# Delta-rule units on one Trainium2 core: masked reads, turns and reads as 64 by 64 products

## The chip, the cores and the metric

The kernel runs on one core of one Trainium2 chip. The metric is the device time of one execution in microseconds; the figure given is the median of several runs. A core has TensorE (matrix products, PE in the profile), VectorE (DVE), ScalarE (ACT), GpSimd (POOL) and SyncE (SP), which here only issues transfers. Products go to PSUM, which has 8 banks of 512 float32 columns on 128 partitions; VectorE and ScalarE carry them on to SBUF.

## The reference

Two blocks follow each other on 1024 tokens of width 1024: a first block (state space mixer, stick-breaking attention, feed-forward) and a second one, whose mixer has a gated linear attention with 4 heads and a delta rule with 8 heads of width 64. The change touches the delta rule:

```python
def _rwkv7_scan(r, decay, k, v, kk, a):
    def step(S, inp):
        r_t, w_t, k_t, v_t, kk_t, a_t = inp
        sa = jnp.einsum('bhvk,bhk->bhv', S, -kk_t)
        S = (S * w_t[:, :, None, :]
             + sa[..., None] * (kk_t * a_t)[:, :, None, :]
             + v_t[..., None] * k_t[:, :, None, :])
        y = jnp.einsum('bhvk,bhk->bhv', S, r_t)
        return S, y
```

After it come, per head, mean and variance over the 64 values of y, a normalisation, a bonus and a gate, and then the product of all heads with `w_out_2`, a residual and a last norm.

## The kernel before, in words

The function `rwkv_units_phase` computes the delta rule and what follows. The 1024 tokens are 8 units of 128, and a unit is two sub-blocks of 64 tokens (`SUB`). A head h = a * 4 + q stands on the partitions of half a (`half(h)`), at place q; `sub(k)` are the partitions or columns of sub-block k. A unit's inputs are five kinds of tiles, read from `parked_units` into `held(c)`: the read vectors (RT_KIND), keys (KT_KIND), removal keys in two forms (KAP_KIND, BT_KIND) and values (VV_KIND), each with channels on partitions and tokens in columns. The inverses of the unit's triangular matrices were made earlier and are fetched into `xt` and `x11`.

One loop, with c from -1 to 7, finishes unit c and prepares unit c + 1; below, pass c is one round of it. The order on each engine is the order of the code, and semaphores connect the engines. On TensorE a pass is:

- `read_values(c)` (line 3574): values times masked reads `rk` into the output sum `y_ps`, bank 6
- `removals(c+1)` (3503): 32 products of 64 by 64 into banks 2 and 3
- `reads_of_removed(c+1)` (3496): 8 products of 128 by 128 (contraction 64) of BT with RT into banks 0 and 1. VectorE multiplies all 128 by 128 entries with a mask (`incl2`) that keeps only the two diagonal 64 by 64 blocks and their causal part, and writes `rb`
- `removal_maps(c)` (3581, 3588): the state's removal map, and `rr_ps` in bank 7
- `turn_values(c+1)` (3527), `reads_of_keys(c+1)` (3496): transposes of keys and values into banks 2 and 3; products of KT with RT, masked into `rk`
- `values(c)` (3595, 3598, 3602): the new states' parts, and the reads of removed values into bank 6
- `means(c-1)` (3627), `turn_keys(c+1)` (3527), `key_parts(c+1)` (3546, 3550)
- `recur(c, 0)` (3614, 3619), `corner(c+1)` (3557), `variances(c-1)` (3631), `recur(c, 1)`, `removed(c+1)` (3566)

Float32 products of four array quarters are possible because a 64 by 64 product takes one half of the rows (partitions of the operands) and one half of the columns (partitions of the result). In the trace a float32 product is two matmul records, a transpose one.

VectorE in a pass: `front` (3699 mask of removals `ak`, 3704 mask `rb`), `maps` (3712, 3717), `front_keys` (3708), `deviation` (3733), `keys` (3722, 3724), `key_values` (3728), the two state updates (3757) with `corner` (3764) between, `result(c-1)` (3741, 3745, 3747), and in passes 1 to 4 `gated(c-1)` (3751, 3753), two operations of 1024 columns for the linear attention's heads. ScalarE: high halves of finished outputs (3831, 3852), copies out of PSUM (3855, 3859, 3868, 3875, 3878), squares (3835) and the root of the variance as logarithm and exponential (3840, 3842). GpSimd makes low halves of outputs (3486, 3478) and cuts the output weights in two (3465 to 3469).

Behind the loop come the output products (3674 to 3676), in three spans of tokens.

Of the kernel before, what the change touches and what calls it, by code (L numbers as in the profile page):

```python
# [14 lines left out]
P = 128  # L15
# [3332 lines left out]
def rwkv_units_phase(nc, S, D, W, plast, L, spare, ssq, merged, parked_h, back, out, s_result, first_unit, s_first):  # L3348
# [6 lines left out]
    with Phase(nc) as ctx:  # L3355
# [11 lines left out]
        rb = part(flat, 4 * SEQ, 2 * SEQ).rearrange("p (s h n) -> p s h n", s=2, h=H)  # L3367
        rk = part(flat, 6 * SEQ, SEQ).rearrange("p (h n) -> p h n", h=H)
# [27 lines left out]
        (s_zero, s_clear, s_rb, s_ak, s_rk, s_zt, s_bt, s_kvt, s_q, s_akv, s_dx, s_w, s_g, s_rr, s_gs, s_yd,  # L3396
         s_rbm, s_akm, s_rkm, s_aam, s_z0, s_tokb, s_tokv, s_qm, s_z1, s_x, s_nw, s_gc, s_rrc, s_state, s_y, s_h, s_hy) = (sem(n) for n in (
            "zero", "clear", "rb", "ak", "rk", "zt", "bt", "kvt", "q", "akv", "dx", "w", "g", "rr", "gs", "yd",
# [17 lines left out]
        y_cols = lambda h: slice((h % RWKV_P) * P, (h % RWKV_P + 1) * P)  # L3416
# [3 lines left out]
        with nc.Block() as block:  # L3420
# [71 lines left out]
            def _(pe):  # L3492
                def wide_products(c, key, kind, out):

                    for h in ORDER:
                        last = nc.tensor.matmul(out[:, h * P:(h + 1) * P], held(c)[half(h), key, h % RWKV_P, :], held(c)[half(h), kind, h % RWKV_P, :],  # L3496
                                                start=True, stop=True)
                    return last
# [18 lines left out]
                def reads_of_removed(c):  # L3517
                    pe.wait_ge(s_nw, c)
                    wide_products(c, BT_KIND, RT_KIND, low_ps).then_inc(s_rb, 1)

                def reads_of_keys(c):
                    pe.wait_ge(s_rbm, c + 1)
                    wide_products(c, KT_KIND, RT_KIND, low_ps).then_inc(s_rk, 1)

                def turned(c, b, kind):
                    for p in range(RWKV_P):
                        last = nc.tensor.transpose(bank(b)[:, p * P:(p + 1) * P], held(c)[:, kind, p, :], S.ident[:, :])  # L3527
                    return last

                def turn_values(c):  # L3530
                    pe.wait_ge(s_akm, c + 1)
                    pe.wait_ge(s_aam, c + 1)
                    turned(c, 2, KT_KIND)
                    turned(c, 3, VV_KIND).then_inc(s_kvt, 1)
# [26 lines left out]
                def removed(c):  # L3561
                    pe.wait_ge(s_x, c + 1)
                    pe.wait_ge(s_z1, c + 1)
                    pe.wait_ge(s_tokb, c + 1)
                    for h in ORDER:
# [4 lines left out]
                def read_values(c):  # L3570
                    pe.wait_ge(s_rkm, c + 1)
                    pe.wait_ge(s_y, c)
                    for h in ORDER:
                        nc.tensor.matmul(y_ps[half(h), y_cols(h)], tkv[:, c % 2, 1, h % RWKV_P, h // RWKV_P, :], rk[:, h, :], start=first(h), stop=False)

                def removal_maps(c):
# [8 lines left out]
                    if c >= 2:  # L3585
                        pe.wait_ge(s_ln, c - 1)
                    for h in ORDER:
                        last = nc.tensor.matmul(rr_ps[half(h), y_cols(h)], nw[:, h, 0, :], rb[:, s, h, :], start=True, stop=True)
                    last.then_inc(s_rr, 1)

                def values(c):
# [9 lines left out]
                    for h in ORDER:  # L3601
                        last = nc.tensor.matmul(y_ps[half(h), y_cols(h)], nw[:, h, 1, :], rb[:, s, h, :], start=False, stop=False)  # L3602
                    last.then_inc(s_hy, 1)

                def recur(c, k):
# [11 lines left out]
                    for h in ORDER:  # L3617
                        at = (h % RWKV_P) * P + k * SUB
                        last = nc.tensor.matmul(y_ps[half(h), at:at + SUB], st[half(h), k, h % RWKV_P, :], rr[half(h), h % RWKV_P, sub(k)],
                                                start=False, stop=(k == 1 and last_(h)))  # L3620
# [3 lines left out]
                def means(c):  # L3624
                    pe.wait_ge(s_y, c + 1)
                    pe.wait_ge(s_rrc, min(c + 2, NUNIT))
                    nc.tensor.matmul(rr_ps, S.same[:, :], y[:, c % 2, :, :].rearrange("p q n -> p (q n)"), start=True, stop=True).then_inc(s_mean, 1)  # L3627

                def variances(c):
                    pe.wait_ge(s_sq, c + 1)  # L3630
                    nc.tensor.matmul(rr_ps, S.same[:, :], sq[:, :, :].rearrange("p q n -> p (q n)"), start=True, stop=True).then_inc(s_var, 1)  # L3631

                for c in range(-1, NUNIT):
# [49 lines left out]
                means(NUNIT - 1)  # L3683
                pe.wait_ge(s_glo, GLA_HEADS)
# [10 lines left out]
            def _(dve):  # L3695
                def front(c):
# [7 lines left out]
                    nc.vector.tensor_tensor(rb[:, s, :, :], by_head(low_ps), S.incl2[:, :].unsqueeze(1).to_broadcast([P, H, P]), ALU.mult).then_inc(s_rbm, 1)  # L3704

                def front_keys(c):
                    dve.wait_ge(s_rk, c + 1)
                    nc.vector.tensor_tensor(rk, by_head(low_ps), S.incl2[:, :].unsqueeze(1).to_broadcast([P, H, P]), ALU.mult).then_inc(s_rkm, 1)

                def maps(c):  # L3710
# [6 lines left out]
                    nc.vector.tensor_tensor(rr[:, :, :], rr_ps.rearrange("p (q n) -> p q n", q=RWKV_P), held(c)[:, RT_KIND, :, :], ALU.add).then_inc(s_rrc, 1)  # L3717
# [369 lines left out]
```

## Time and profile before

| | |
|---|---|
| median of 3 runs | 2276.01 us (2269.75 to 2276.87) |
| the profiled execution | 2273.69 us |
| its span | 2271.9 us, 43790 instructions |
| TensorE busy | 2167.5 us (95%) |
| VectorE busy | 1574.2 us (69%) |
| ScalarE busy | 993.5 us (44%) |
| mean granted clock of TensorE | 0.987 of 2.4 GHz |
| the unit loop | about 2006 to 2173 us of the span |

Busy time is the sum of what an engine executed; matmuls are pipelined, so a busy TensorE can still be one that works below its peak. What bounds a stretch is read from the chain of waits: from the last instruction back, at each step, to whatever released it. "issue" there is time in which the engine waited for nothing that the profile shows.

### The profile page before, as it was taken

Reading aid. Unit: us, or ns where it says so; the run is one execution under the profiler, and the core shown is the slowest. Engines: PE = TensorE matmul, PEld = TensorE weight load, DVE = VectorE, ACT = ScalarE, POOL = GpSimd, SP = SyncE. Lnnn points to the kernel's source line nnn. Section 1 sums busy time; section 2 is a strip of 40 time slices with the busy share of each in tenths; the row PEclk is TensorE's granted clock in tenths of the full one; section 3 lists DMA queues with packets and bytes.
Section 4 is the critical chain, followed back from the end, with each engine's and each line's share of the span. In section 5 each row is a group of like instructions: output and inputs, shape, how many; then the busy total and the mean of one; then the engine's idle time right before and its main releaser. Section 6 shows DMA issues by size and latency. Waiting matters only on the chain. (4 is left out here: it accounts for less than half of the span.)

```text
span 2271.9 us, 43790 instructions
## 1 busy us (share of the span) xinstructions
PE 2167.5 (95%) x18260; PEld 1377.7 (61%) x18260; DVE 1574.2 (69%) x2017; ACT 993.5 (44%) x1739; POOL 605.8 (27%) x379
## 2 busy tenths in 40 slices
PE   7999989999999899899999999999999999989998
PEld 4666665556666566566666665448644445568746
DVE  6876887988888755787777774247787576246654
ACT  3226765666666543524444443235553332224321
POOL 3555673100000220073333331000155532101160
PEclk9999999999999999999999999999999999999999
DMA  3113214667777632111111113326424522033412
GB/s 133 47 56 96 83 66 75 132 131 141 147 136 147 135 105 77 44 56 42 56 57 57 57 53 120 102 68 208 139 90 125 167 93 89 14 98 99 167 61 75
DMA packets 287947, 218.32 MB, mean 96 GB/s; under 512 B 203328, under 2 KB 253696, under 8 KB 286352
## 3 DMA queue, kind: packets, MB, share of 16 engines
q1 hardware_dynamic: 287760, 215.64, 34.9%
q8 instruction: 139, 2.28, 0.4%
q14 instruction: 48, 0.39, 0.1%
HBM read 145.77 MB, written 25.76 MB: 75 GB/s over the span
## 5 line engine op out<-in xcount | busy, mean ns | idle before, releaser
L1499 DVE TENSOR_TENSOR_SCAN att_left<-att_left,att_unseen_prefix 16x16 f32<-16x16 f32 (+5 forms) x144 | 175.5, 1258 | 16.6 <-ACT att_left L1327 16.4
L2886 PE MATMUL ps<-second_x_hi,whi_z 128*128 128x512 f16 (+1 forms) x480 | 179.2, 373 | 2.6 <-DVE second_x_lo L1714 1.4
L1221 PE MATMUL ps<-x_hi,whi_z 128*128 128x348 f16 x560 | 175.8, 314 | 4.4 <-DVE att_q L1431 4.4
L2888 PE MATMUL ps<-second_x_hi,wlo_z 128*128 128x512 f16 (+1 forms) x480 | 178.9, 373 | 0.0
L2887 PE MATMUL ps<-second_x_lo,whi_z 128*128 128x512 f16 (+1 forms) x480 | 178.8, 373 | 0.0
L1223 PE MATMUL ps<-x_hi,wlo_z 128*128 128x348 f16 x560 | 174.7, 312 | 0.0
L1222 PE MATMUL ps<-x_lo,whi_z 128*128 128x348 f16 x560 | 174.5, 312 | 0.0
L1341 ACT ACTIVATE att_left_split<-att_left 128x256 f16<-128x256 f32 (+7 forms) x128 | 87.3, 682 | 142.1 <-DVE att_left L1499 128.1
L2189 PE MATMUL ps<-x_lo,whi_z 128*128 128x342 f16 x432 | 133.2, 308 | 0.0
L2188 PE MATMUL ps<-x_hi,whi_z 128*128 128x342 f16 x432 | 132.9, 308 | 0.0
L2190 PE MATMUL ps<-x_hi,wlo_z 128*128 128x342 f16 x432 | 132.7, 307 | 0.0
L2855 POOL TENSOR_TENSOR wlo_z<-wraw_z,whi_z 128x1024 f16<-128x1024 f32 x28 | 65.9, 2354 | 180.0 <-ACT whi_z L3071 180.0
L1456 DVE SCALAR_TENSOR_TENSOR att_left_split<-att_left,att_left_split 128x256 f16<-128x256 f32 (+7 forms) x128 | 96.9, 757 | 0.2
L3071 ACT ACTIVATE whi_z<-wraw_z 128x1024 f16<-128x1024 f32 x28 | 29.6, 1056 | 133.5 <-PE ps L2888 117.1
L219 PE MATMUL ps<-x_hi,whi_xbc 128*128 128x348 f16 x264 | 82.6, 313 | 4.6 <-DVE x_lo L487 4.6
L2886 PEld LDWEIGHTS ps<-second_x_hi,whi_z 128*128 128x128 f16 x480 | 46.9, 98 | 62.3 <-issue 6.5
L1268 PE MATMUL ps<-att_left_turned,att_v_tokens 128*64 128x128 f16 x1728 | 64.4, 229 | 19.7 <-DMA att_left_turned<-att_left_split 10.2
L221 PE MATMUL ps<-x_hi,wlo_xbc 128*128 128x348 f16 x264 | 82.5, 312 | 0.0
L220 PE MATMUL ps<-x_lo,whi_xbc 128*128 128x348 f16 x264 | 82.4, 312 | 0.0
L1327 ACT ACTIVATE att_left<-ps 16x16 f32<-16x16 f32 (+5 forms) x144 | 79.1, 595 | 4.4 <-PE ps L1237 4.4
L1221 PEld LDWEIGHTS ps<-x_hi,whi_z 128*128 128x128 f16 x560 | 54.5, 97 | 43.2 <-issue 15.6
L2887 PEld LDWEIGHTS ps<-second_x_lo,whi_z 128*128 128x128 f16 x480 | 47.0, 98 | 53.7 <-issue 3.9
(655 smaller groups left out, 6226.5 us busy)
## 6 DMA issues: line engine op xcount, KB each, us to landing
wraw_z<-in_w_second SPq DMA_DIRECT2D x30, 512.0 KB, 4.1
wraw_z<-in_w_up SPq DMA_DIRECT2D x26, 512.0 KB, 3.6
wraw_z<-in_w_qkv SPq DMA_DIRECT2D x24, 512.0 KB, 4.5
wraw_z<-in_w_down SPq DMA_DIRECT2D x20, 512.0 KB, 3.5
raw_down<-in_w_down SPq DMA_DIRECT2D x20, 512.0 KB, 4.1
seg<-dt_a_sums SPq DMA_DIRECT2D x18, 512.0 KB, 5.3
wraw_z<-in_w_up SPq DMA_DIRECT2D x36, 256.0 KB, 3.3
second_work<-parked_units SPq DMA_DIRECT2D x7, 1280.0 KB, 7.3
```

What stands on the lines that cost most here:

```text
L1221: nc.tensor.matmul(lin_ps(g), hi, xhi, start=(kb == 0), stop=False)
L1222: nc.tensor.matmul(lin_ps(g), hi, xlo, start=False, stop=False)
L1223: last = nc.tensor.matmul(lin_ps(g), lo, xhi, start=False, stop=(kb == DB - 1))
L1341: last = nc.scalar.activation(left_part(e, 0, P * t.j), of_head(t, a, 0, P * t.j), ACT.Copy, scale=PSCALE)
L1456: last = nc.vector.scalar_tensor_tensor(low_, of_head(t, a, 0, P * t.j), PSCALE, high, ALU.mult, ALU.subtract)
L1499: nc.vector.tensor_tensor_scan(x, x, unseen, 1.0, ALU.mult, ALU.max).then_inc(s_scan, 1)
L2188: nc.tensor.matmul(out, hi, xhi, start=begin, stop=False, skip_group_check=True)
L2189: nc.tensor.matmul(out, hi, xlo, start=False, stop=False, skip_group_check=True)
L2190: of_block = nc.tensor.matmul(out, lo, xhi, start=False, stop=stop, skip_group_check=True)
L2886: nc.tensor.matmul(out, hi, xhi, start=(j == 0), stop=False)
L2887: nc.tensor.matmul(out, hi, xlo, start=False, stop=False)
L2888: return nc.tensor.matmul(out, lo, xhi, start=False, stop=(j == DB - 1))
```

## The change

All large products of the unit loop that had a dimension of 128 become 64 by 64 products, and results move to other banks.

- The masked reads (`own_products` in place of `wide_products`) compute only the two diagonal 64 by 64 blocks of each head: 16 calls in place of 8, into the low half of banks 0 and 1, and the masks on VectorE work on 512 columns in place of 1024.
- The turns are products with an identity of 64 by 64, 16 calls in place of 4 transposes, both kinds side by side in the same two banks.
- `read_values`, the `rr` part of `removal_maps` and the reads of removed values (now `read_removed`) contract over one sub-block, 16 calls in place of 8. `y_ps` and `rr_ps` share banks 6 and 7, one bank for each sub-block.
- Means and variances go to banks 0 and 1 (bank 7 for the last unit). So the turns of the keys wait for the deviation, the variances for the copy of the turned keys, and `removed` for the logarithm.
- In a pass `reads_of_keys` stands ahead of `turn_values`, and the means ahead of `read_removed`.

```diff
-        low_ps, high_ps = (S.ps[:, b:b + 2, :].rearrange("p a n -> p (a n)") for b in (0, 2))
+        low_ps = S.ps[:, 0:2, :].rearrange("p a n -> p (a n)")
+        own_ps = S.ps[:, 0:2, 0:RWKV_P * SUB].rearrange("p a (q n) -> p a q n", n=SUB)
+        turned_ps = lambda b, j: S.ps[:, b:b + 2, j * RWKV_P * SUB:(j + 1) * RWKV_P * SUB].rearrange("p a (q n) -> p a q n", n=SUB)
...
-        y_ps, rr_ps = bank(6), bank(7)
+        y_ps, rr_ps = (S.ps[:, 6:8, o * RWKV_P * SUB:(o + 1) * RWKV_P * SUB].rearrange("p k (q n) -> p k q n", n=SUB) for o in range(2))
+        mean_ps, var_ps = (lambda c, b=b: bank(7 if c == NUNIT - 1 else b) for b in range(2))
...
-                def wide_products(c, key, kind, out):
-
-                    for h in ORDER:
-                        last = nc.tensor.matmul(out[:, h * P:(h + 1) * P], held(c)[half(h), key, h % RWKV_P, :], held(c)[half(h), kind, h % RWKV_P, :],
-                                                start=True, stop=True)
+                def own_products(c, key, kind):
+
+                    for k, h in kh:
+                        last = nc.tensor.matmul(own_ps[sub(k), h // RWKV_P, h % RWKV_P, :], held(c)[half(h), key, h % RWKV_P, sub(k)],
+                                                held(c)[half(h), kind, h % RWKV_P, sub(k)], start=True, stop=True)
                     return last
...
-                def turned(c, b, kind):
-                    for p in range(RWKV_P):
-                        last = nc.tensor.transpose(bank(b)[:, p * P:(p + 1) * P], held(c)[:, kind, p, :], S.ident[:, :])
+                def turned(c, b, j, kind):
+                    for k, h in kh:
+                        last = nc.tensor.matmul(turned_ps(b, j)[sub(k), h // RWKV_P, h % RWKV_P, :], held(c)[half(h), kind, h % RWKV_P, sub(k)],
+                                                S.ident[half(h), half(h)], start=True, stop=True)
                     return last
...
                 def turn_keys(c):
                     pe.wait_ge(s_rkm, c + 1)
-                    turned(c, 0, KAP_KIND).then_inc(s_zt, 1)
-                    turned(c, 1, BT_KIND).then_inc(s_bt, 1)
+                    if c >= 2:
+                        pe.wait_ge(s_dev, c - 1)
+                    turned(c, 0, 0, KAP_KIND)
+                    turned(c, 0, 1, BT_KIND).then_inc(s_bt, 1)
...
-                    for h in ORDER:
-                        nc.tensor.matmul(y_ps[half(h), y_cols(h)], tkv[:, c % 2, 1, h % RWKV_P, h // RWKV_P, :], rk[:, h, :], start=first(h), stop=False)
+                    for k, h in kh:
+                        nc.tensor.matmul(y_ps[half(h), k, h % RWKV_P, :], tkv[sub(k), c % 2, 1, h % RWKV_P, h // RWKV_P, :], rk[sub(k), h, :],
+                                         start=first(h), stop=False, skip_group_check=True)
...
+                def read_removed(c):
+                    pe.wait_ge(s_rrc, c + 1)
+                    for k, h in kh:
+                        last = nc.tensor.matmul(y_ps[half(h), k, h % RWKV_P, :], nw[sub(k), h, 1, :], rb[sub(k), c % 2, h, :], start=False, stop=False,
+                                                skip_group_check=True)
                     last.then_inc(s_hy, 1)
...
                 def means(c):
                     pe.wait_ge(s_y, c + 1)
-                    pe.wait_ge(s_rrc, min(c + 2, NUNIT))
-                    nc.tensor.matmul(rr_ps, S.same[:, :], y[:, c % 2, :, :].rearrange("p q n -> p (q n)"), start=True, stop=True).then_inc(s_mean, 1)
+                    if c + 2 < NUNIT:
+                        pe.wait_ge(s_rkm, c + 3)
+                    nc.tensor.matmul(mean_ps(c), S.same[:, :], y[:, c % 2, :, :].rearrange("p q n -> p (q n)"), start=True, stop=True).then_inc(s_mean, 1)
...
                     if ahead:
+                        reads_of_keys(c + 1)
                         turn_values(c + 1)
-                        reads_of_keys(c + 1)
                     if now:
-                        values(c)
+                        new_states(c)
                     if c >= 1:
                         means(c - 1)
+                    if now:
+                        read_removed(c)
```

The places of instructions on TensorE, first before. This is the middle of a pass with c of 2 or more, from `read_values` to `key_parts`; `second_work` holds the unit's inputs, `z` stands for `rb`, `rk`, `nw` or the removal tile, `ffn_out` for `tkv` and `xt`.

```order
L3574 MATMUL ps<-z,ffn_out 64x128 x8
L3503 MATMUL ps<-second_work 64x64 x32
L3496 MATMUL ps<-second_work 128x128 x8
L3581 MATMUL ps<-ru_tok_removal,z 64x64 x16
L3588 MATMUL ps<-z 64x128 x8
L3527 MATMUL ps<-ident,second_work 128x128 x8
L3496 MATMUL ps<-second_work 128x128 x8
L3595 MATMUL ps<-ffn_out 64x64 x16
L3598 MATMUL ps<-z,ru_tok_removal 64x64 x16
L3602 MATMUL ps<-z 64x128 x8
L3627 MATMUL ps<-wraw_z,same_chunk 128x512
L3527 MATMUL ps<-ident,second_work 128x128 x8
```

Every second group stands at another tile shape than the one ahead of it, and the read of the keys stands behind the turn of the values. The same place on TensorE in the changed kernel:

```order
L3582 MATMUL ps<-z,ffn_out 64x64 x16
L3506 MATMUL ps<-second_work 64x64 x32
L3499 MATMUL ps<-second_work 64x64 x16
L3590 MATMUL ps<-ru_tok_removal,z 64x64 x16
L3595 MATMUL ps<-z 64x64 x16
L3499 MATMUL ps<-second_work 64x64 x16
L3530 MATMUL ps<-ident,second_work 64x64 x32
L3603 MATMUL ps<-ffn_out 64x64 x16
L3606 MATMUL ps<-z,ru_tok_removal 64x64 x16
L3639 MATMUL ps<-wraw_z,same_chunk 128x512
L3613 MATMUL ps<-z 64x64 x16
L3530 MATMUL ps<-ident,second_work 64x64 x32
```

All but the means have one tile shape; the read of the keys (the second 3499) moved ahead of the turn of the values, and the means (3639) ahead of the reads of the removed values (3613). VectorE's order is the same, with two operations half as wide.

## Rows read from the trace of the kernel before

**Rows 1.** The page: busy time, share and instructions of the engines.
```profile
PE 2167.5 (95%) x18260; PEld 1377.7 (61%) x18260; DVE 1574.2 (69%) x2017; ACT 993.5 (44%) x1739; POOL 605.8 (27%) x379
```

**Rows 2.** Stretches: length, busy and instructions per engine, clock, DMA share, GB/s.
```profile
2084.30:2104.20 19.90, 19.03 (x436) 16.18 (x436) 13.86 (x25) 9.12 (x13) 3.46 (x3) 1.00 0.35 99
...
2124.80:2149.80 25.00, 22.72 (x458) 19.38 (x460) 12.95 (x25) 7.11 (x10) 2.82 (x2) 0.93 0.78 288
```

**Rows 3.** The chain that ended last, one unit: start, us, engine, what.
```profile
2095.70 0.70 ACT ru_y_rs L3840
...
2101.35 1.24 DVE second_work L3753
...
2104.29 0.74 PE ps L3527 x5
```

**Rows 4.** Timeline of TensorE in one unit: start, us, engine, line, operation, tiles.
```profile
2105.29 1.16 PE L3496 MATMUL ps<-second_work 64*128 64x128 f32 x16
...
2106.38 0.69 PE L3595 MATMUL ps<-ffn_out 64*64 64x64 f32 x32
...
2107.47 1.09 PE L3602 MATMUL ps<-z 128*64 128x128 f32 x16
...
2108.49 1.13 PE L3627 MATMUL ps<-wraw_z,same_chunk 128*128 128x512 f32 x2
...
2109.46 1.04 PE L3527 MATMUL ps<-ident,second_work 128*128 128x128 f32 x8
...
2110.42 1.12 PE L3546 MATMUL ps<-ffn_out,ru_removal 64*64 64x32 f32 x32
...
2118.39 1.09 PE L3574 MATMUL ps<-z,ffn_out 128*64 128x128 f32 x16
...
2119.41 1.16 PE L3503 MATMUL ps<-second_work 64*64 64x64 f32 x64
...
2120.51 1.16 PE L3496 MATMUL ps<-second_work 64*128 64x128 f32 x16
...
2121.60 0.69 PE L3581 MATMUL ps<-ru_tok_removal,z 64*64 64x64 f32 x32
...
2122.22 1.09 PE L3588 MATMUL ps<-z 128*64 128x128 f32 x16
...
2124.88 1.07 PE L3527 MATMUL ps<-ident,second_work 128*128 128x128 f32 x8 [1.56 <-ACT ru_removal L3855]
```

**Rows 5.** The same timeline, two of VectorE and one of ScalarE.
```profile
2109.66 0.69 DVE L3733 SCALAR_TENSOR_TENSOR wraw_z<-ps,wraw_z 128x512 f32<-128x512 f32 x1 [1.94 <-PE ps L3627]
...
2115.44 0.69 ACT L3840 ACTIVATE ru_y_rs<-ps,gn_eps 128x512 f32<-128x512 f32 x1 [3.46 <-PE ps L3631]
...
2123.08 0.68 DVE L3699 TENSOR_TENSOR ru_ak<-ps,excl 128x512 f32<-128x512 f32 x1
```

**Rows 6.** Waits of TensorE from 2020 to 2172 us: total, times, longest.
```profile
PE ps L3614 <- issue: 1.8, 2, 1.4
```

**Rows 7.** Timeline of TensorE at the longest stall.
```profile
2145.01 0.46 PE L3581 MATMUL ps<-ru_tok_removal,z 64*64 64x64 f32 x16 [2.03 <-issue]
```

**Rows 8.** Half-microsecond stretches: length, TensorE busy, clock, DMA share, GB/s.
```profile
2146.50:2147.00 0.50, 0.50 (x4) 0.50 0.29 107
...
2149.00:2149.50 0.50, 0.50 (x8) 0.50 0.00 0
```

**Rows 9.** Timeline: first unit, and the ScalarE step behind two later variances.
```profile
2015.02 1.12 PE L3546 MATMUL ps<-ffn_out,ru_removal 64*64 64x32 f32 x32
...
2136.03 0.69 ACT L3840 ACTIVATE ru_y_rs<-ps,gn_eps 128x512 f32<-128x512 f32 x1 [3.46 <-PE ps L3631]
...
2159.16 0.69 ACT L3840 ACTIVATE ru_y_rs<-ps,gn_eps 128x512 f32<-128x512 f32 x1 [3.46 <-PE ps L3631]
```

**Rows 10.** Timeline behind the last unit: VectorE held up, GpSimd later.
```profile
2181.27 2.93 DVE L3741 SCALAR_TENSOR_TENSOR wraw_z<-wraw_z,params,ru_y_rs 128x128 f32<-128x128 f32 x4 [3.65 <-ACT ru_y_rs L3842]
...
2186.84 1.16 POOL L3486 TENSOR_TENSOR second_x_lo<-wraw_z,second_x_hi 128x512 f16<-128x512 f32 x1 [3.58 <-ACT second_x_hi L3831]
```

More of the change, by code:

```diff
@@ L3366, in rwkv_units_phase @@
         tkv = mid_w.rearrange("p (s j q a n) -> p s j q a n", s=2, j=2, q=RWKV_P, a=2)
-        rb = part(flat, 4 * SEQ, 2 * SEQ).rearrange("p (s h n) -> p s h n", s=2, h=H)
-        rk = part(flat, 6 * SEQ, SEQ).rearrange("p (h n) -> p h n", h=H)
+        rb = part(flat, 4 * SEQ, SEQ).rearrange("p (s h n) -> p s h n", s=2, h=H)
+        rk = part(flat, 5 * SEQ, SEQ // 2).rearrange("p (h n) -> p h n", h=H)
         nw = part(flat, 7 * SEQ, SEQ).rearrange("p (h a n) -> p h a n", h=H, a=2)
@@ L3584, in removal_maps, with new_states @@
                     pe.wait_ge(s_rrc, c)
[L3585 to L3588, printed above, removed]
+                    for k, h in kh:
+                        last = nc.tensor.matmul(rr_ps[half(h), k, h % RWKV_P, :], nw[sub(k), h, 0, :], rb[sub(k), s, h, :], start=False, stop=True,
+                                                skip_group_check=True)
                     last.then_inc(s_rr, 1)
-                def values(c):
+                def new_states(c):
                     s = c % 2
@@ L3600, in values @@
                     last.then_inc(s_h, 1)
-                    for h in ORDER:
-                        last = nc.tensor.matmul(y_ps[half(h), y_cols(h)], nw[:, h, 1, :], rb[:, s, h, :], start=False, stop=False)
+                def read_removed(c):
+                    pe.wait_ge(s_rrc, c + 1)
+                    for k, h in kh:
+                        last = nc.tensor.matmul(y_ps[half(h), k, h % RWKV_P, :], nw[sub(k), h, 1, :], rb[sub(k), c % 2, h, :], start=False, stop=False,
+                                                skip_group_check=True)
                     last.then_inc(s_hy, 1)
@@ L3617, in recur @@
                     for h in ORDER:
-                        at = (h % RWKV_P) * P + k * SUB
-                        last = nc.tensor.matmul(y_ps[half(h), at:at + SUB], st[half(h), k, h % RWKV_P, :], rr[half(h), h % RWKV_P, sub(k)],
-                                                start=False, stop=(k == 1 and last_(h)))
+                        last = nc.tensor.matmul(y_ps[half(h), k, h % RWKV_P, :], st[half(h), k, h % RWKV_P, :], rr[half(h), h % RWKV_P, sub(k)],
+                                                start=False, stop=last_(h), skip_group_check=True)
                     if k:
@@ L3625, in means @@
                     pe.wait_ge(s_y, c + 1)
-                    pe.wait_ge(s_rrc, min(c + 2, NUNIT))
-                    nc.tensor.matmul(rr_ps, S.same[:, :], y[:, c % 2, :, :].rearrange("p q n -> p (q n)"), start=True, stop=True).then_inc(s_mean, 1)
+                    if c + 2 < NUNIT:
+                        pe.wait_ge(s_rkm, c + 3)
+                    nc.tensor.matmul(mean_ps(c), S.same[:, :], y[:, c % 2, :, :].rearrange("p q n -> p (q n)"), start=True, stop=True).then_inc(s_mean, 1)
                 def variances(c):
                     pe.wait_ge(s_sq, c + 1)
-                    nc.tensor.matmul(rr_ps, S.same[:, :], sq[:, :, :].rearrange("p q n -> p (q n)"), start=True, stop=True).then_inc(s_var, 1)
+                    if c + 2 < NUNIT:
+                        pe.wait_ge(s_tokb, c + 3)
+                    nc.tensor.matmul(var_ps(c), S.same[:, :], sq[:, :, :].rearrange("p q n -> p (q n)"), start=True, stop=True).then_inc(s_var, 1)
                 for c in range(-1, NUNIT):
```

41 lines of the change are left out of this document (23 added, 18 removed).

## The prediction, as it was put on record

> **What bounds the kernel now.** I read the page first, then the table of stretches, then the chain of waits, then the timeline of one unit on each engine. The page says that TensorE is busy 95% of the span [rows 1], but the change touches only the last loop over eight units, some 165 us of 2271.9. In a stretch of one unit TensorE is busy 19.03 of 19.90 us and VectorE 13.86 [rows 2], so one would call it bound by TensorE. The chain says otherwise for some units. Unit by unit there are two cases.
>
> In loop passes 2 to 5 (pass c works on unit c and prepares unit c+1) the chain leaves TensorE. It goes from ScalarE's logarithm of the variance (line 3840) at 2095.70 through VectorE's normalising and its two wide operations for the other head family (3751, 3753), which end at 2102.59, through the mask of the next unit and a ScalarE copy, back to TensorE at 2104.29 [rows 3]. The next logarithm starts at 2115.44 [rows 5], so the loop is 19.74 us: 8.59 away from TensorE, 11.15 on it. TensorE idles before line 3527 in these passes, 1.56 us in one [rows 4]. In passes 0, 1 and 6 the wide operations don't stand there, and TensorE sets the pace. So a saving on TensorE counts in full in three passes, and in four only where it lies between line 3527 and the variances.
>
> **The price of a product.** In rows 4 the start of one group to the start of the next is what a group costs. 32 calls on 64 by 64 quarters (3503) go from 2119.41 to 2120.51, 1.10 us; 16 such calls (3581) from 2121.60 to 2122.22, 0.62 us. The difference is 0.48 us for 16 calls, and 0.14 us is left for the change of tile shape ahead of each. Eight wide calls cost about twice that: 3496 takes 1.09, 3602 takes 1.02, 3574 takes 1.02 [rows 4].
>
> **TensorE, part by part, per unit.** Reads of values and removals after them: 2118.39 to 2120.51, 2.12, become 0.14 + 0.48 + 0.96 = 1.58, saves 0.54. Masked read of removals (3496): 1.09 to 0.48, saves 0.61. The maps (3581) lose their shape change, 0.14. Line 3588, 1.02 back to back as 3602 is, to 0.48, saves 0.54. Masked read of keys: 1.09 to 0.48, saves 0.61. Turns: eight transposes at 128 by 128 took 1.00 (2104.29 to 2105.29) and 0.96 (2109.46 to 2110.42); 32 calls of a quarter cost 0.96, saves 0.04 and nothing. States (3595 and 3598): 1.09 to 0.96, saves 0.13. Line 3602: 1.02 to 0.14 + 0.48, saves 0.40. The sum is 3.0 us of 19 per unit [rows 3, 4].
>
> The Trainium skill's page TensorEngine Tiling (Array Packing), section Instruction Overhead, says that each matmul carries about 60 cycles, so that a dimension of 64 gains nothing by being cut. As an estimate by that page, 32 records of 25 ns would make a group 0.80 us instead of 0.48, and nearly all of the 3.0 us would be gone over nine such groups. The trace disagrees: 0.48 us for a group of 32 records.
>
> **The wait that is added.** Means now write bank 0, which the turns of the keys write next, so those turns wait for VectorE's deviation. From the start of the means to the start of the deviation is 1.17 us (2108.49 to 2109.66) and it lasts 0.69 [rows 4, 5], with a hop of 0.06 in all 1.92. TensorE has 0.97 of means and 0.62 of reads in that time, 1.59, and then waits 0.33. Queued behind are the turns and all that follows in the pass. The other new waits are covered: the means' wait for the masked keys (VectorE is two operations of 0.68 ahead by then, against 1.9 us of turns and states), the variances' for a copy that ends over 2 us earlier, the removal product's for the logarithm (0.69, under the recurrence's 0.93 beside it); if that last cover went, it would cost 0.3 us a pass, and I count that in the low end.
>
> **VectorE and ScalarE.** The two masks fall from 1024 to 512 columns; a mask of 512 takes 0.68 [rows 5]. In the passes that TensorE bounds they are hidden either way. In the others the first is on the path now, since the read of the keys is put ahead of the turn and waits for it. The evictions that only change their stride keep their element count; I take them at no change, and a bound of plus or minus 0.1 each. The SP queue's waits are on operations that come earlier or at the same place; it has whole passes to spare.
>
> **The loop of passes 2 to 5, new.** 6.89 us from logarithm to mask (2095.70 to 2102.59), unchanged. Two masks, 0.68 each, and hops: the read of the keys starts at 8.39. Then 0.48, turns 0.96, states 0.96: 10.79. Shape change 0.14 and the 1.92 above: 12.85. Turns 0.96, and from line 3546 to the logarithm 5.02 as now (2110.42 to 2115.44): 18.83. Against 19.74 that is 0.9 us, four times 3.6 us [rows 3 to 5]. Most of the 3.0 us is therefore given back as idle time of TensorE: it finishes its front part 2.95 + 3.02 = 5.97 after the logarithm (2115.44 to 2118.39, then the groups above) and waits 2.4 us, against 1.56 or less now.
>
> **The other passes.** Pass 0 has no means: 3.0 us. Pass 1 up to its variances, and the stretch from the variances of pass 5 to those of pass 6, 3.0 less 0.33 each: 2.7 and 2.7. The first unit: its chain is two masks and two turns shorter, but line 3546, now at 2015.02, needs a transfer that I can't place; the gain is 0 to 1.9, I take the middle, 1.1 [rows 9]. The last: some 1.0 us shorter, but the end hangs on a GpSimd operation at 2186.84, behind VectorE's normalising, which a GpSimd operation of the output weights holds up to 2.93 us [rows 10]. That release doesn't move with the unit, so I keep 0.7 (bounds 0 and 1.0). Ideal sum: 1.1 + 3.0 + 2.7 + 3.6 + 2.7 + 0.7 = 13.8 us.
>
> **What takes some back.** First the clock. After a stall of 2.03 us at 2145 [rows 7] the granted clock stood at 0.50, 1.2 GHz, from 2146.5 to 2149.5 [rows 8], costing about 1.6 us of work; the idle 1.56 us in rows 4 left it at 1.00 [rows 2, 4]. The new idle time of 2.4 us lies beyond the one that fell. Each fall costs up to 1.6 us just where TensorE is on the path. Bounds are no fall and four; I take two or three, 4.0 us. Second the instruction supply. The stalls that wait for nothing the profile shows, 1.8 and 2.03 us [rows 6, 7], come where transfers are dense (DMA share 0.78 in that stretch). A unit goes from 436 matmul records [rows 2] to 628: five groups of 8 calls become 16, with two records a call, 80 more, and four turns go from 4 records to 32, 112 more. If such stalls grow with the records, by 44%, it is 1.7 us more; bounds are 3.8 less and 10 more.
>
> Net 13.8 - 4.0 - 1.7 = 8.1 us. From the profiled execution's 2273.7 that gives 2265.6, from the median of the three runs, 2276.0, it gives 2267.9; those runs go down to 2269.75, so I start from 2274 and forecast 2266.
>
> **Rivals.** (B) The clock holds, and the long stall with its slow stretch, 3.6 us between the variances of passes 5 and 6 (2136.03 to 2159.16 is 23.13 us where 19.5 would do [rows 9]), falls elsewhere or vanishes, as the instruction stream has other lengths. For it: stalls of this kind come in few passes. Against: the same burst of transfers is there. 13.8 + 3.6 gives 17.4 us off: counted like the forecast from 2274, 2257. Chance 0.25. (C) The clock falls in all four passes and once more, and the stalls double: 13.8 - 8.0 - 3.8 = 2 us, 2272. Chance 0.16. (D) Slower: TensorE runs out of instructions in every unit. The quarters want 64 records (128 instructions with the weight loads) in 0.96 us in one row after another; now such stretches are short. The place is the seven passes' bursts of unit transfers; from 2 us of new stall in each of seven passes the gain is gone, and with a clock fall behind each, 3.6 us, it is 25 against 13.8: 2285. Against: 3503 and 3581 run at that rate now without one in most passes. Chance 0.06. (E) The new groups don't run on four quarters at once. Line 3546, on two of the quarters, is busy 1.12 us for 32 records where 3581 is busy 0.69 [rows 4]. At twice 0.48 nine groups cost 4.3 us more per unit, TensorE 1.3 more than now in three passes, the loop of the four 1.5 more: 10 us slower, 2284. Against: their rows of the array write different banks, as in 3581. Chance 0.03.
>
> My forecast has 0.50, for gains of 5 to 12 us. About 0.3% or 6.8 us is what a measurement can tell. Three quarters of the forecast's chance and all of B are beyond it: 0.63 faster. The rest of the forecast and C: 0.28 the same. D and E: 0.09 slower. The range of 2256 to 2275 holds the forecast, C and most of B.
>
> **What would show it.** Right: groups of 16 calls 0.48 us apart; 628 records per unit; logarithm to logarithm 18.8 us in passes 2 to 5, near 20.4 where the clock fell; TensorE idle about 2.4 us ahead of the read of the keys, released by VectorE's mask, and 0.3 us ahead of the second turns, released by the deviation; pass 0 shorter by 3 us. Wrong: groups at 0.8 or 0.96 us; idle time of TensorE elsewhere, with no releaser and over 1 us, in most passes; a clock below 1.00 in none or all of the passes; an eviction with the new stride longer by tenths.

## The result, and the profile after

The changed kernel takes 2301.55 us (median of 4 runs, 2295.95 to 2305.17), the one before 2273.98 in the same comparison: ratio 1.0118, 95% interval 1.0103 to 1.0133. It is slower by 27.6 us where 8 us less were forecast, and outside the range of 2256 to 2275.

The page of the profile after: span, busy times, granted clock in tenths over 40 slices, and the queue of instruction loads (packets, MB, share).

```profile
span 2303.4 us, 46873 instructions
...
PE 2167.2 (94%) x19796; PEld 1381.6 (60%) x19796; DVE 1562.6 (68%) x2017; ACT 995.3 (43%) x1739; POOL 610.0 (26%) x379
...
PEclk9999999999999999999999999999999999988899
...
q8 instruction: 151, 2.47, 0.5%
```

TensorE is busy as long as before [rows 1] and the span is 31.5 us longer. Nearly all of it lies in the unit loop; behind the loop the two traces differ by 0.2 us (92.0 and 92.2). From its first product to the last logarithm of a variance the loop took 173.8 us before (2006.05 to 2179.89) and takes 200.4 now (2010.77 to 2211.17), 26.6 more. When the loop begins differs by up to 7 us between profiled executions of kernels that are the same up to there, so below a loop is compared with a loop. In passes 2 to 5 the logarithms stood 20.44, 19.75, 19.74 and 20.59 us apart before and stand 22.27, 25.49, 24.48 and 24.77 apart now, where 18.83 was forecast.

The timeline of TensorE in one pass of the changed kernel (start, us, line, tiles, count, idle time ahead with its releaser), from the read of removals on. It answers to [rows 4].

```profile
2098.18 0.65 PE L3590 MATMUL ps<-ru_tok_removal,z 64*64 64x64 f32 x32
...
2098.65 0.65 PE L3595 MATMUL ps<-z 64*64 64x64 f32 x32
...
2101.45 0.69 PE L3499 MATMUL ps<-second_work 64*64 64x64 f32 x32 [2.15 <-DVE z L3721]
...
2101.96 1.11 PE L3530 MATMUL ps<-ident,second_work 64*64 64x64 f32 x64
...
2102.89 0.65 PE L3603 MATMUL ps<-ffn_out 64*64 64x64 f32 x32
...
2103.36 0.30 PE L3606 MATMUL ps<-z,ru_tok_removal 64*64 64x64 f32 x8
...
2104.72 0.58 PE L3606 MATMUL ps<-z,ru_tok_removal 64*64 64x64 f32 x24 [1.06 <-issue]
...
2105.23 1.13 PE L3639 MATMUL ps<-wraw_z,same_chunk 128*128 128x512 f32 x2
...
2106.29 0.69 PE L3613 MATMUL ps<-z 64*64 64x64 f32 x32
...
2107.23 1.16 PE L3530 MATMUL ps<-ident,second_work 64*64 64x64 f32 x64 [0.25 <-DVE wraw_z L3751]
...
2108.18 0.30 PE L3552 MATMUL ps<-ffn_out,ru_removal 64*64 64x32 f32 x4
...
2110.95 1.70 PE L3552 MATMUL ps<-ffn_out,ru_removal 64*64 64x32 f32 x28 [2.46 <-issue]
...
2112.36 2.05 PE L3556 MATMUL ps<-ffn_out,ru_ak 64*64 64x64 f32 x32
```

Two things are to be seen. The groups cost what the sum had: 3590 and 3595 follow each other in 0.47 us, the read of the keys (3499) takes 0.51 from 2101.45 to 2101.96 with its shape change already paid, a turn of 32 calls 0.93 to 0.95. And between them stand stalls that no semaphore ends: 1.06 us inside line 3606, 2.46 us inside line 3552. Both lie in the middle of a group that waits for nothing. Then 3552 and 3556 run slower: 28 records in 1.41 us, where all 32 of the same group (3546) took 0.96 before.

The waits of TensorE between 2012 and 2205 us, in total, times and longest:

```profile
PE ps L3499 <- DVE z L3721: 10.9, 5, 3.0
PE ps L3530 <- issue: 7.1, 3, 3.6
PE ps L3552 <- issue: 6.9, 3, 2.5
PE ps L3603 <- issue: 3.4, 2, 1.8
PE ps L3606 <- issue: 2.1, 3, 1.1
PE ps L3595 <- issue: 2.1, 2, 1.1
PE ps L3506 <- issue: 2.0, 1, 2.0
PE ps L3530 <- DVE wraw_z L3751: 1.5, 6, 0.3
```

Stalls with no releaser ("issue") add up to 24.6 us in 15 places; before there were 3.8 us in three [rows 6, 7]. The wait for VectorE's masked `rb` (first row) and for the deviation (last row, 0.3 at most, six times) are those of the prediction.

The clock around the 2.46 us stall: stretch, length, TensorE busy with its number of records, granted clock, DMA share, GB/s.

```profile
2107.00:2109.00 2.00, 1.25 (x68) 1.00 0.95 206
2109.00:2111.00 2.00, 0.05 (x3) 0.92 0.02 2
2111.00:2113.00 2.00, 2.00 (x39) 0.50 0.04 8
2113.00:2115.00 2.00, 2.00 (x44) 0.50 0.00 0
2115.00:2117.00 2.00, 2.00 (x44) 0.50 0.00 0
2117.00:2119.00 2.00, 2.00 (x27) 0.87 0.04 8
```

The granted clock was 1.00 up to the stall and 0.50, 1.2 GHz, behind it, and rose again at 2117.5. Over the loop's time it stood low for 52.1 us after, in ten stretches, and 6.8 before, in two. Of the ten, one lies in the first unit (there is one before, too), six begin at or behind a stall with no releaser, and three at or behind a wait for the mask (at 2080.0, 2127.8 and 2151.7).

### The profile page after: what moved, and what is told of

Its sections match the earlier page's. It is cut to its first block and busy times, and to the rows that moved or that the text cites. A ratio compares the mean times of both kernels' runs of the same rounds, so it can differ in the third digit from the quotient of the medians.

```text
span 2303.4 us, 46873 instructions
## 1 busy us (share of the span) xinstructions
PE 2167.2 (94%) x19796; PEld 1381.6 (60%) x19796; DVE 1562.6 (68%) x2017; ACT 995.3 (43%) x1739; POOL 610.0 (26%) x379
## 5 line engine op out<-in xcount | busy, mean ns | idle before, releaser
L1499 DVE TENSOR_TENSOR_SCAN att_left<-att_left,att_unseen_prefix 16x16 f32<-16x16 f32 (+5 forms) x144 | 175.5, 1259 | 17.1 <-ACT att_left L1327 16.9
L1268 PE MATMUL ps<-att_left_turned,att_v_tokens 128*64 128x128 f16 x1728 | 64.1, 228 | 19.7 <-DMA att_left_turned<-att_left_split 9.8
L2131 POOL TENSOR_TENSOR down_squares<-wraw_z 128x512 f32<-128x512 f32 x18 | 27.5, 1528 | 200.5 <-DMA wraw_z<-in_w_up 196.4
```

Of the source, the lines that this page charges most:

```text
L1499: nc.vector.tensor_tensor_scan(x, x, unseen, 1.0, ALU.mult, ALU.max).then_inc(s_scan, 1)
```

## The experiments

Theory S: TensorE takes instructions faster in 64 by 64 groups than they are delivered, stalls, and the clock falls behind the stalls. Rivals: P, the products, banks or the order cost time themselves; T, only the unit transfers delay the instruction loads. "Loop" is measured as above; stalls are TensorE's idle times of over 0.2 us that no releaser ends, and "low clock" is the time within the loop at 1.2 GHz. These three come from one profiled execution each, the time from all runs. Each ratio is against the kernel before in its own comparison, where that took 2273.57 to 2274.08 us.

| kernel | records per unit | time, us | ratio to before, 95% | loop, us | stalls, us | low clock, us |
|---|---|---|---|---|---|---|
| before | 436 | 2273.98 | | 173.8 | 3.8 | 6.8 |
| contractions only | 484 | 2276.42 | 1.0008 (0.9998 to 1.0017) | 171.6 | 3.7 | 6.8 |
| turns back | 516 | 2279.78 | 1.0023 (1.0011 to 1.0035) | 176.6 | 14.8 | 20.5 |
| turns back, old order | 516 | 2281.74 | 1.0026 (1.0016 to 1.0036) | 180.2 | 13.4 | 27.3 |
| turns only | 548 | 2287.44 | 1.0063 (1.0044 to 1.0082) | 186.4 | 10.8 | 13.7 |
| changed | 628 | 2301.55 | 1.0118 (1.0103 to 1.0133) | 200.4 | 24.6 | 52.1 |

The stalls do not follow the number of records alone: 548 have 10.8 us of them, 516 have 14.8.

**The turns as transposes again (e1).** The rest as changed.

```diff
-                def turned(c, b, j, kind):
-                    for k, h in kh:
-                        last = nc.tensor.matmul(turned_ps(b, j)[sub(k), h // RWKV_P, h % RWKV_P, :], ...,
-                                                S.ident[half(h), half(h)], start=True, stop=True)
+                def turned(c, b, kind):
+                    for p in range(RWKV_P):
+                        last = nc.tensor.transpose(bank(b)[:, p * P:(p + 1) * P], held(c)[:, kind, p, :], S.ident[:, :])
```

> The changed kernel with the four turns of a unit as 128 by 128 transposes again (4 matmul records each in place of 32), all else as changed: 516 records per unit in place of 628, before had 436. Theory S (instruction supply: TensorE consumes instructions in its 64 by 64 groups faster than they arrive, stalls, and the clock falls behind the stalls): stalls with no releaser fall from 24.7 us to under 12, time 2268 to 2284, far nearer to before than to the changed kernel. Theory P (the 64 by 64 products, new banks or order cost the time themselves): the turns take the same TensorE time either way, so the time stays within 4 us of the changed kernel, 2298 to 2304.

Measured 2279.78 us, ratio 1.0023 (1.0011 to 1.0035). 21.8 of the 27.6 us are back, though the turns take the same TensorE time either way; the stalls are 14.8 us where under 12 were expected. Theory P is out for the turns. This run also shows the predicted loop without its clock fall. TensorE and ScalarE from one logarithm to the next:

```profile
2078.82 0.69 ACT L3857 ACTIVATE ru_y_rs<-ps,gn_eps 128x512 f32<-128x512 f32 x1 [4.24 <-PE ps L3644]
...
2084.34 0.52 PE L3589 MATMUL ps<-ru_tok_removal,z 64*64 64x64 f32 x21 [0.35 <-issue]
...
2086.95 0.69 PE L3499 MATMUL ps<-second_work 64*64 64x64 f32 x32 [1.57 <-DVE z L3720]
...
2095.47 0.51 PE L3555 MATMUL ps<-ffn_out,ru_ak 64*64 64x64 f32 x11 [1.05 <-issue]
...
2098.97 0.69 ACT L3857 ACTIVATE ru_y_rs<-ps,gn_eps 128x512 f32<-128x512 f32 x1 [4.72 <-PE ps L3644]
```

The loop is 20.15 us with stalls of 0.35 and 1.05 us in it. Without the 1.05 and the 0.35 it would be 18.75 at best; the prediction had 18.83. The 0.35 need not be on the path, as it lies ahead of the wait for VectorE; with it, the loop would be 19.1. e8 below shows the loop without any stall.

**Only the turns changed (e2).** The kernel before with the quarter turns; VectorE waits for both turns of the keys.

```diff
-                    turned(c, 2, KT_KIND)
-                    turned(c, 3, VV_KIND).then_inc(s_kvt, 1)
+                    turned(c, 2, 0, KT_KIND)
+                    turned(c, 2, 1, VV_KIND).then_inc(s_kvt, 1)
```

> The kernel before with only the four turns of a unit as 64 by 64 products (548 records per unit in place of 436; VectorE waits for both key turns before its first copy). TensorE's work stays the same by the price of a group. Theory S: new stalls with no releaser, 5 to 12 us of them, and 2280 to 2292. Theory P with the masked reads or new banks at fault: as before, 2272 to 2278.

Measured 2287.44 us, ratio 1.0063 (1.0044 to 1.0082), stalls 10.8 us. A part that by the price of its groups costs nothing costs 14 us, and it moves no bank of the sums and no masked read. In the loop it is 12.6 us: 7.0 more of stalls, at most 3.4 for the 6.9 us more of low clock (half of them), and 2.2 that are left. Those may be VectorE's later copy of the first turn; this run doesn't separate it.

**Few transfers (e3 on the changed kernel, e4 on the one before).** From unit 3 on one row of the unit's inputs is fetched, from unit 2 on one row of the inverses, so later units compute with earlier inputs.

```diff
-                        sp.dma_start(fx[:, s, :, :, :], D.units[c]).then_inc(s_in[s], 16)
+                        if c < 3:
+                            sp.dma_start(fx[:, s, :, :, :], D.units[c]).then_inc(s_in[s], 16)
+                        else:
+                            sp.dma_start(fx[0:1, s, 0, 0, :], D.units[c][0:1, 0, 0, :]).then_inc(s_in[s], 16)
```

> The changed kernel with the loop's transfers of unit inputs cut to one row from unit 3 on and of the inverses from unit 2 on (so it computes later units with earlier inputs). Theory S in the form that supply is bound by its own rate: most stalls stay, at least 15 of 24.7 us, and 2290 or more. Rival T (the instruction loads are late only because the unit transfers fill the DMA engines): stalls under 6 us and 2262 to 2270.

> The kernel before with the same transfers cut. Theory S: stalls of 3.8 us stay or shift, 2270 to 2275. Rival T: the stalls vanish, 2266 to 2270. Beside the changed kernel with few transfers it gives what the change is worth without unit transfers: S says still slower by 15 us or more, T says faster by 5 to 14 us.

Measured 2285.07 us (ratio to the full kernel before 1.0047, 1.0028 to 1.0066) and 2270.01 us (0.9986, 0.9976 to 0.9997). Cutting the transfers gives the changed kernel 16.5 us and the one before 3.6 to 4. Theory T explains about half of the 27.6 us: with few transfers in both, the changed one is still 15 us slower, with 16.4 us of stalls. The time lies below what S alone had expected, 2290 or more. The 4 MB of the residual, late in the loop, move in both as before. So both count: the rate of the supply, and transfers in its way.

**The supply by itself (e5).** The kernel before, with repeats in the first unit that change no result.

```diff
+                    if c == 0:
+                        for _ in range(60):
+                            chunk_products(c, KT_KIND, KAP_KIND, ak_ps)
                     chunk_products(c, KT_KIND, KAP_KIND, ak_ps)
...
+                    if c == 0:
+                        for _ in range(20):
+                            wide_products(c, BT_KIND, RT_KIND, low_ps)
                     wide_products(c, BT_KIND, RT_KIND, low_ps).then_inc(s_rb, 1)
```

> The kernel before with the supply measured by itself in the first unit, by repeats that change nothing: 60 times a group of 16 calls on 64 by 64 quarters (32 matmul records and 32 weight loads each) ahead of the removals, then 20 times the group of 8 wide calls (16 and 16 records) ahead of the masked read. No transfer that the groups wait for lies in between. Theory S: the quarters take 45 us or more for the 60 groups where 28.8 would do at 0.48 us each, with stalls at even distances of about 256 instructions, though no unit transfer runs; the wide ones take 1.09 each, 21.8 us, without a stall. Theory P: 28.8 us and no stall. Theory T (unit transfers delay the instruction loads): no stall in either.

It is one execution of 2348.33 us, read for its trace and not for its time. Start, us, what and idle time ahead on TensorE (the last row is the wide products):

```profile
2008.72 6.36 PE L3503 MATMUL ps<-second_x_lo 64*64 64x64 f32 x292 [1.09 <-PEq L2791]
2016.76 2.10 PE L3503 MATMUL ps<-second_x_lo 64*64 64x64 f32 x128 [1.69 <-issue]
2023.25 3.51 PE L3503 MATMUL ps<-second_x_lo 64*64 64x64 f32 x128 [4.39 <-issue]
...
2042.52 2.93 PE L3503 MATMUL ps<-second_x_lo 64*64 64x64 f32 x128 [1.92 <-issue]
2046.54 3.69 PE L3503 MATMUL ps<-second_x_lo 64*64 64x64 f32 x128 [1.09 <-issue]
...
2054.03 2.10 PE L3503 MATMUL ps<-second_x_lo 64*64 64x64 f32 x128 [1.38 <-issue]
2057.79 2.10 PE L3503 MATMUL ps<-second_x_lo 64*64 64x64 f32 x128 [1.67 <-issue]
2061.28 2.10 PE L3503 MATMUL ps<-second_x_lo 64*64 64x64 f32 x128 [1.39 <-issue]
2064.76 2.10 PE L3503 MATMUL ps<-second_x_lo 64*64 64x64 f32 x128 [1.38 <-issue]
...
2068.84 19.03 PE L3496 MATMUL ps<-second_x_lo 64*128 64x128 f32 x336
```

This run gave the clearest answer. The quarters run 128 records, stall, and run 128 records again. At their closest the starts are 3.48 us apart (2057.79, 2061.28, 2064.76): 2.10 us busy and 1.38 us stalled, with no transfer to speak of, as the next table shows. They are not always so close with idle DMA queues: from 2027.27 to 2038.51 they are 3.75 apart, then three times 4.02. 128 records with their weight loads are 256 instructions, and the queue of instruction loads moves 16 KB a packet (2.28 MB in 139 packets on the page before). Before the first stall 292 records ran; one instruction packet began and ended in that time, at 2009.85, so about 164 were at hand (an estimate: 292 less its 128). The 21 wide groups, 336 records in 18.98 us, have no stall; that is 0.90 us a group.

```profile
2054.00:2068.20 14.20, 8.38 (x512) 1.00 0.02 5
2068.90:2087.70 18.80, 18.80 (x338) 1.00 0.01 3
```

The loads themselves are in the trace. From 2057.79 to 2064.76, two blocks, the DMA engines moved two packets, both of instructions:

```profile
DMA packets 2, 0.03 MB, mean 5 GB/s; under 512 B 0, under 2 KB 0, under 8 KB 0
...
q8 instruction: 2, 0.03, 1.6%
```

That is one packet of 16 KB for each block of 256 instructions, and the blocks next to these have one each as well. So the stalls are waits for instruction packets.

While the unit's transfers ran (DMA share 0.89 from 2015 to 2024) one stall was 4.39 us. The changed kernel shows the same ahead of its 2.46 us stall: from 2104.8 to 2108.4 the DMA queues moved 1.23 MB of data and not one instruction packet, and the next one began between 2108.4 and 2108.5, as TensorE ran dry:

```profile
q1 hardware_dynamic: 1323, 1.23, 102.0%
```

Theory P is out, T is only the second part. The 60 groups and the two of the removals, 1984 records, took from 2008.72 to 2068.84, 60.1 us, against 29.8 at 0.48 for 32.

**Only the contractions (e6).** The kernel before with `read_values`, the `rr` part and `read_removed` as quarters; masked reads wide, turns transposed.

```diff
-                    for h in ORDER:
-                        nc.tensor.matmul(y_ps[half(h), y_cols(h)], tkv[:, c % 2, 1, h % RWKV_P, h // RWKV_P, :], rk[:, h, :], start=first(h), stop=False)
+                    for k, h in kh:
+                        nc.tensor.matmul(y_ps[half(h), k, h % RWKV_P, :], tkv[sub(k), c % 2, 1, h % RWKV_P, h // RWKV_P, :], rk[sub(k), h, sub(k)],
+                                         start=first(h), stop=False, skip_group_check=True)
```

> The kernel before with only read_values, the rr part and read_removed as 64 by 64 products, with their banks, waits and the means ahead of read_removed; masked reads stay wide, turns stay transposes: 484 records per unit. Ideal gain by the price of a group 1.5 us per unit where TensorE sets the pace and 0.1 to 0.4 in the other passes, about 5 us; theory S: stalls grow from 3.8 to 6 to 10 us, so 2270 to 2276, no clear difference from before. Theory P: slower than before by 4 us or more.

Measured 2276.42 us, ratio 1.0008 (0.9998 to 1.0017): no clear difference, and 3.7 us of stalls where 6 to 10 were expected. The new banks, the deviation's wait and the moved means are all in it; by the interval they cost 4 us at most, and are no cause of the 27.6. They are not free: passes 2 to 4 took 20.2 to 20.6 us where the kernel before, without a stall there (e9 below), takes 19.7, with TensorE waiting 0.33 us for the mask ahead of the means and 0.25 for the deviation in each.

**The old order (e7).** As e1, with the turn of the values ahead of the read of the keys.

```diff
-                        reads_of_keys(c + 1)
                         turn_values(c + 1)
+                        reads_of_keys(c + 1)
```

> The changed kernel with transposes and with the turn of the values ahead of the read of the keys again: the same 516 records as the variant with the turns back, only the order differs, and a tile shape change more. Theory S: dense groups are spread more evenly, 10 to 15 us of stalls, 2274 to 2284, within 4 us of the variant with the turns back. If the new order were a cause of its own, 5 us or more faster than that variant.

Measured 2281.74 us, ratio 1.0026 (1.0016 to 1.0036), against 1.0023 for e1: with the turns as transposes, the order is no cause.

**Spread transfers (e8 on e1, e9 on the kernel before, e11 on the changed one).** The inputs of a unit come in five pieces, one kind each, and the inverses behind them, each behind an event of the pass.

```diff
-                        sp.dma_start(fx[:, s, :, :, :], D.units[c]).then_inc(s_in[s], 16)
+                        for j, (event, count) in enumerate(((s_rrc, c - 1), (s_rrc, c - 1), (s_hy, c - 1), (s_q, c), (s_gs, 2 * c - 3))):
+                            if c >= 2:
+                                sp.wait_ge(event, count)
+                            sp.dma_start(fx[:, s, j, :, :], D.units[c][:, j, :, :]).then_inc(s_in[s], 16)
...
                     for k in range(2):
+                        if c >= 2:
+                            sp.wait_ge(*((s_dx, c) if k == 0 else (s_yd, c - 1)))
```

> The variant with the turns back as transposes, and the transfer of a unit's inputs cut in five pieces of 256 KB whose issue is spread over the pass (behind the masked maps, the reads of removed values, the key parts, the recurrence), the inverses behind corner and recurrence. Theory S with transfers as the second part (an instruction load that meets a full burst of transfers lands late): stalls fall from 14.8 us to under 10, 2268 to 2277, faster than the variant without the spread by 3 us or more. If only the supply's own rate counts: no change, 2277 to 2283.

> The kernel before with the same spread of its transfers. Stalls of 3.8 us fall to 1 to 3, 2270 to 2275: at most the 3.6 us that cutting the transfers gave. If only the supply's own rate counts: as before.

> The changed kernel with the transfers of a unit spread as in the two variants before. 628 records per unit at 3.48 us for 128 are 17.1 us, close to what a pass takes: stalls fall from 24.6 us to some 15, 2282 to 2292, as far as cutting the transfers brought it (2285) but not to the kernel before. If transfers alone were the cause it would come to 2268 or less.

Measured: e8 2271.14 us, 0.9990 (0.9978 to 1.0003), 8.6 us less than e1 (7.6 by the ratios), stalls 9.8 us; e9 2269.68, 0.9986 (0.9977 to 0.9995), stalls 1.7 us and 3.4 us of low clock, at the loop's start; e11 2289.08, 1.0057 (1.0037 to 1.0078), stalls 20.0 us where some 15 were expected. Of these 20.0, 7.9 are two stalls (2.93 and 4.96) behind the issue of the residual's 4 MB. Spreading takes off about half of what the changed kernel lost, as cutting the transfers did, and leaves the rest. In e8 one stall is left that is longer than the others, while the 4 MB of the residual are on their way:

```profile
PE ps L3607 <- issue: 3.5, 1, 3.5
```

e8 also has what e1 lacked, passes that run free. Three of the times between logarithms are 18.88, 18.88 and 18.89 us; in the first two a stall of 0.68 and 1.13 us lies ahead of the wait for the mask and costs nothing, in the third, between these rows, there is none:

```profile
2093.69 0.69 ACT L3862 ACTIVATE ru_y_rs<-ps,gn_eps 128x512 f32<-128x512 f32 x1 [3.46 <-PE ps L3649]
...
2112.58 0.69 ACT L3862 ACTIVATE ru_y_rs<-ps,gn_eps 128x512 f32<-128x512 f32 x1 [3.46 <-PE ps L3649]
```

The fourth is 21.23, with a wait of 2.98 us for the mask and the clock at 0.50 for 3.4 us behind it.

**Few transfers with the turns back (e10).** The edit of e3 on e1.

> The variant with the turns back, with the loop's transfers cut to one row (later units computed from earlier inputs), as for the changed kernel and the one before. It bounds what spreading can give. Records per unit 516, at the measured 3.48 us for 128 records 14.0 us a unit, below the 18.8 of the pass: stalls under 8 us, 2264 to 2272, faster than the kernel before with few transfers or equal to it. If the products or banks cost time themselves: 2275 or more.

Measured 2268.56 us, ratio 0.9982 (0.9971 to 0.9993), stalls 7.9 us. It is the bound for spreading the unit transfers with 516 records; e8 comes within 2.6 us of it.

**A version that beats both (e12).** e8, and the residual in eight pieces over the last two passes.

```diff
-                        sp.dma_start(back, parked_h).then_inc(s_back, 16)
...
+                    if c == NUNIT - 1:
+                        for b, (event, count) in enumerate(((s_yd, c - 1), (s_rrc, c), (s_hy, c), (s_q, c + 1), (s_dx, c + 1), (s_yd, c), (s_rrc, c + 1), (s_yd, c + 1))):
+                            sp.wait_ge(event, count)
+                            sp.dma_start(back[:, b, :], parked_h[:, b, :]).then_inc(s_back, 16)
```

> The variant with the turns back and the spread transfers, and the 4 MB transfer of the residual (back) in eight pieces spread over the last two passes. The 3.49 us stall at 2145 us of the variant without this lies in that transfer; gone with it: 2266 to 2271, faster than the kernel before by 2 to 6 us. If the stall has another cause: 2271 as that variant.

Measured 2267.63 us, ratio 0.9963 (0.9950 to 0.9977), faster than the kernel before (2275.18 in this comparison) by 7.5 us. Its waits from 2012 to 2205 us:

```profile
PE ps L3507 <- DVE z L3728: 6.1, 4, 2.2
PE ps L3597 <- issue: 2.5, 3, 1.4
...
PE ps L3602 <- issue: 1.6, 1, 1.6
PE ps L3610 <- issue: 1.5, 1, 1.5
...
PE ps L3507 <- issue: 0.9, 2, 0.5
...
```

Stalls with no releaser are 7.0 us, none over 1.6. The loop is 167.5 us against 173.8. The kernel before with the unit's and the residual's transfers spread was not run, so the 7.5 us are not all shown to be the quarters'. With the unit's alone (e9) it has 0.9986; the two ratios differ by 0.0023, some 5 us, and that holds the spread residual too.

## Why the prediction was wrong, point by point

- **The price of a product was right.** Groups of 16 calls stand 0.47 us apart in the timeline after, and a unit has 628 records. The Trainium skill's page TensorEngine Tiling (Array Packing), section Instruction Overhead, by whose about 60 cycles a matmul the prediction estimated 0.80 us, doesn't hold for the group as such. Rival E is out. The copies with a new stride are no longer either: ScalarE's of the turned keys and values takes 1.024 us, 1.023 before.
- **The loop of passes 2 to 5** was right where it ran free: 18.88 and 18.89 us in e8, against 18.83. But the prediction took 19.74 as the time before for all four of these passes, and only two had it; pass 5 had 20.59, and has 21.23 in e8. The ideal gain of 13.8 us is shown for three passes, 0.9 us each. No run shows it whole, as no variant is free of stalls; the 6.8 us for all up to the variances of pass 1 appear in none of the variants traced (from the loop's start to the first logarithm 49.5 us before, 47.6 in e10, 48.2 in e8, 49.5 in e12).
- **The new waits** were right: 0.3 us for the deviation, and TensorE's wait for VectorE's mask, 2.15 us in three passes and 2.99 in the fourth (2.4 forecast).
- **The step that failed is the instruction supply.** The prediction scaled 3.8 us of stalls by the 44% more records and took 1.7 us more, 10 at most. Measured are 20.8 us more. Stalls don't grow in step with the count: they begin where the demand passes the supply. By e5 the supply is 128 records in 3.48 to 4.02 us and a run of quarters wants them in about 1.9 (0.48 for 32). Before, such runs were 64 records long, with wide groups between them in which the supply caught up. Now nearly the whole pass is one run: 628 records need 17.1 us of supply at 3.48, and 18.4 at 3.75, in a pass of 18.8 by the forecast, and a burst of transfers takes some of it (in e5 it made one stall 3.0 us longer than 1.38).
- **The clock** is the second term that was too small: 4.0 us for two or three falls of 3 us each. There are ten low stretches, 52.1 us, and five of them last 6.8 us or more. The loop's excess is 26.6 = -13.8 + 20.8 + 19.6. The last term is what is left for the clock, if the 13.8 were there and every stall counts in full; half of the 45.3 us more at the low clock, 22.7, is its upper bound. That part is worked out and was not tried by itself.
- **The rival that came true is D**, given 0.06: TensorE runs out of instructions. Its price was too low, 25 us taken back where 40.4 were (20.8 + 19.6), so 2285 for 2301.55, less than half of the loss. Its place, the bursts of unit transfers, was half of it: with few transfers 16.4 us of stalls stay (e3). Its objection, that 3503 and 3581 ran at that rate without a stall, rested on runs of 64 and 32 records, shorter than what was at hand (about 164 in e5).
- The wait for VectorE with its idle time, which was to cause the clock's falls, did so in places: at three of the ten falls in the changed kernel, and ahead of pass 5's variances in e8. Not every such wait was followed by one: behind the 2.15 us at 2101.45 the clock stayed at 1.00. Which idle time is too long was not settled.

## What to carry to other kernels

Cutting a product in quarters to save array time multiplies the instructions; count records per microsecond over a whole pass, not over one group, and compare it with what a long run gets. On this kernel 128 matmul records with their weight loads came every 3.48 us at best and every 4.02 at times, and a burst of transfers delayed that by up to 3 us more. A stall with no releaser in the middle of a group, where no semaphore is waited for, is the mark of it, and the packets of the instruction queue in that stretch confirm it; first take back the cuts that save no array time (here the turns, 21.8 us), then spread the transfers that stand in the way (8.6 us).

## What was not expected of the hardware

- Instruction blocks in e5: 128 matmul records and one 16 KB instruction packet, 3.48 us with a stall of 1.38 at the closest, 3.75 to 4.02 in other places; 292 records ahead of the first stall; 4.39 us of stall while a 1280 KB transfer ran.
- When the supply is the bound, the slow clock costs little. In e5 the blocks at 2042.52 and 2046.54 took 2.93 and 3.69 us instead of 2.10, and the stalls behind them shrank to 1.09 and 0.33; the starts stayed 4.02 us apart, against 3.75 in the blocks ahead of them.
- A TensorE busy for 8.38 of 14.20 us in e5 kept a granted clock of 1.00 throughout (2054.0 to 2068.2), and so it did from 2027.3 to 2042.5, busy for 8.35 of 15.20 us; behind the same rhythm it then fell to 0.50 from 2043.5 to 2050.3, after a stall of 1.92 us. In the changed kernel it fell at the end of a single stall of 2.46 us.
